# The end of an encoder layer: moved outputs, a wait split over eight chunks, and an embedding product behind the second gate product

## The reference

```python
    x = x + rms_norm(m @ w_out, post_g)

    x = x + jax.nn.sigmoid(x @ w_pg) * (p_i @ w_pe)
    return x
```

## Time and profile before

| | us |
|---|---|
| median of 3 runs | 1331.39 (1331.17 to 1331.68) |
| the profiled execution | 1330.88 |
| its span, first to last instruction | 1329.1 |
| PE busy | 1305.7 |
| DVE busy | 726.3 |
| ACT busy | 596.4 |
| POOL busy | 354.2 |

### The profile page before, as it was taken

One profiled execution on the slowest core, in us unless ns is written; L12 is line 12 of the kernel. 1 busy time (PEld: TensorE's weight loads), 2 busy tenths in 40 slices (PEclk: granted clock), 3 DMA queues, 4 the chain that ended last, 5 costly groups with the idle time before them and its releaser, 6 DMA issues.

```text
span 1329.1 us, 17627 instructions
## 1 busy us (share of the span) xinstructions
PE 1305.7 (98%) x6600; PEld 1065.2 (80%) x6600; DVE 726.3 (55%) x1356; ACT 596.4 (45%) x1152; POOL 354.2 (27%) x239
## 2 busy tenths in 40 slices
PE   9999999999999999999999999999999999999898
PEld 6788877888888778788888788888877888887787
DVE  6354645546522677786633435555547337436865
ACT  6355455553222577676422245555554223224442
POOL 4122212122434311130244512221211443216000
PEclk9999999999999999999999999999999999999999
DMA  6211112101111200000111211111101114424111
GB/s 214 64 41 41 44 38 57 52 32 52 49 48 32 66 31 17 17 17 24 46 53 37 79 52 44 48 50 46 32 24 41 48 40 149 142 79 145 48 40 56
DMA packets 26866, 74.29 MB, mean 56 GB/s; under 512 B 2936, under 2 KB 4856, under 8 KB 26656
## 3 DMA queue, kind: packets, MB, share of 16 engines
q1 hardware_dynamic: 26784, 73.19, 17.4%
HBM read 68.95 MB, written 4.23 MB: 55 GB/s over the span
## 4 chain that ended last, share of the span: by engine, by line
PE 88%; DVE 6%; ACT 3%; issue 2%; DMA 1%; POOL 1%; SPq 0%; ACTq 0%; DVEq 0%; POOLq 0%
PE ps L984 18%; PE ps L1003 14%; PE ps L1340 13%; PE ps L1578 6%; PE ps L1225 6%; PE ps L1392 5%; PE ps L1640 4%; PE ps L1381 2%; PE ps L1023 2%; PE ps L1162 2%; PE ps L1078 2%; PE ps L1310 2%; PE ps L1456 2%; PE ps L1193 1%; PE ps L1284 1%
## 5 line engine op out<-in xcount | busy, mean ns | idle before, releaser
L776 POOL TENSOR_TENSOR w_lo<-stage,w_hi 128x1024 fp32r<-128x1024 f32 (+2 forms) x84 | 190.1, 2264 | 578.9 <-ACT w_hi L1715 578.9
L1715 ACT CAST w_hi<-stage 128x1024 fp32r<-128x1024 f32 (+2 forms) x92 | 91.3, 993 | 198.8 <-PE ps L984 126.4
L2343 DVE TENSOR_TENSOR pt_lo<-ps,pt_hi 128x512 fp32r<-128x512 f32 (+2 forms) x160 | 97.1, 607 | 80.5 <-ACT pt_hi L2079 40.2
L1003 PE MATMUL ps<-h_hi,w_hi 128*128 128x512 f32 x272 | 110.3, 405 | 0.0
L984 PE MATMUL ps<-h_hi,w_hi 128*128 128x512 f32 x352 | 109.0, 391 | 1.2 <-POOL w_lo L776 1.2
L984 PE MATMUL ps<-h_lo,w_hi 128*128 128x512 f32 x352 | 108.5, 389 | 0.0
L984 PE MATMUL ps<-h_hi,w_lo 128*128 128x512 f32 x352 | 108.4, 389 | 0.0
L1340 PE MATMUL ps<-h_hi,w_hi 128*128 128x512 f32 x256 | 106.8, 417 | 0.0
L1003 PE MATMUL ps<-h_hi,w_lo 128*128 128x512 f32 x272 | 106.2, 391 | 0.0
L1003 PE MATMUL ps<-h_lo,w_hi 128*128 128x512 f32 x272 | 106.1, 390 | 0.0
L1340 PE MATMUL ps<-h_hi,w_lo 128*128 128x512 f32 x256 | 100.4, 392 | 0.0
(11 more groups left out here) (456 smaller groups left out, 3131.9 us busy)
## 6 DMA issues: line engine op xcount, KB each, us to landing
stage<-in_w_gates SPq DMA_DIRECT2D x24, 512.0 KB, 3.6
stage<-in_w_qkvg_a SPq DMA_DIRECT2D x19, 512.0 KB, 4.3
stage<-in_w_qkvg_c SPq DMA_DIRECT2D x16, 512.0 KB, 3.7
m<-in_x_tok SPq DMA_DIRECT2D x8, 512.0 KB, 6.1
stage<-in_w_branch SPq DMA_DIRECT2D x8, 512.0 KB, 3.7
y_plain<-in_x_tok SPq DMA_DIRECT2D x8, 512.0 KB, 3.6
stage<-in_w_pg SPq DMA_DIRECT2D x16, 256.0 KB, 3.5
out<-y_plain SPq DMA_DIRECT2D x16, 256.0 KB, 2.0
```

The costliest lines, as they stand in the source:

```text
L776: nc.gpsimd.tensor_tensor(dst, stage[:, staged, 0:width], f32(hi), ALU.subtract).then_inc(w_ready, 1)
L1003: done = mm(ps[:, half_bank(T), :], w[:, slot, k * P:(k + 1) * P], h[:, k, g * SEQ:(g + 1) * SEQ], start=k == 0 and part == 0, stop=k == K ...
L1715: nc.scalar.copy(dst, stage[:, staged, 0:width]).then_inc(w_hi_done, 1)
L2343: sub = lambda out, whole, hi: nc.vector.tensor_tensor(out, whole, f32(hi), ALU.subtract)
```

## The change

On PE the single wait for the right half of w_pg goes. Product e = 2 waits chunk by chunk instead, and all four full gate products go through their chunks in the order PG1_ORDER. In the seven products `gate_embedding(p, 0)` moves from behind the third product to behind the second. On ACT the tanh of e = 1 moves from behind the copies of all weight sums to behind those of c = 0, and the tanh of e = 3 moves ahead of the third unit part and the save of a21. On DVE output 0 moves ahead of weight sums 1, output 1 ahead of weight sums 2 and 3, and output 3 ahead of the third unit part.

```diff
                 pe.wait_ge(o_ready, LEAD + max(e - 1, 0))
-                for k in range(KC):
+                for n, k in enumerate(PG1_ORDER):
+                    if e == 2:
+                        pe.wait_ge(pg1_ready, LEAD + n + 1)
                     for part, (a, w) in enumerate([(a_hi, g_hi), (a_hi, g_lo), (a_lo, g_hi)]):
                         mm(ps[:, c, :], a[:, k * P:(k + 1) * P], w[:, k * 512:(k + 1) * 512],
-                           start=k == 0 and part == 0, stop=k == KC - 1 and part == 2)
+                           start=n == 0 and part == 0, stop=n == KC - 1 and part == 2)
...
-                for i in range(3):
+                for i in range(2):
                     gate_product(p, i)
                 gate_embedding(p, 0)
-                for i in range(3, 5):
+                for i in range(2, 5):
                     gate_product(p, i)
...
             for e in range(PLAIN_EMBEDS):
-                if e == 2:
-                    pe.wait_ge(pg1_ready, LEAD + KC)
                 if e < 3:
                     turn_x2(e + 1)
                 embed(e)
...
                 for which in (4, 2, 3):
                     sums_hi(which, c)
-            embed_tanh(1)
+                if c == 0:
+                    embed_tanh(1)
             unit_hi(0, 0)
             unit_hi(0, 1)
             for t in (2, 3):
                 p_hi(t)
             embed_tanh(2)
+            embed_tanh(3)
             unit_hi(0, 2)
             save_a21(0)
-            embed_tanh(3)
...
             gate_weight_sums(0)
+            output(0, 2)
             gate_weight_sums(1)
-            output(0, 2)
+            output(1, 3)
             gate_weight_sums(2)
             gate_weight_sums(3)
             sums_lo(4)
-            output(1, 3)
             sums_lo(2)
             unit_low(0, 0)
             unit_low(0, 1)
             for t in (2, 3):
                 p_low(t)
             output(2, 2)
+            output(3, 3)
             unit_low(0, 2)
-            output(3, 3)
```

## The result

| | kernel before | changed kernel |
|---|---|---|
| median of 22 runs each, us | 1331.16 | 1333.68 |
| lowest to highest, us | 1330.47 to 1332.35 | 1332.45 to 1334.66 |
| ratio to before (95% interval) | | 1.0018 (1.0012 to 1.0024) |
| profiled execution, us | 1330.88 | 1333.37 |
| its span, us | 1329.1 | 1331.6 |

The first view is what PE waited for in the changed kernel, from 1200 us to the end (engine and line, what it waited for: us in total, times, longest). It answers the earlier trace rows. Lines behind the edits have moved by one to two: the seven products are now L1642, the full gate products L1614, take is L3017, and the output's two operations are L3025 and L3028.

A forecast was written before the change was run, and what follows sets the result against it. TensorE (PE), busy 98% of the span, was taken as the bound. Gains 1.9 + 0.6 against 3.05 added gave 0.55 slower; with 1.4 for the clock, 1331.4 + 0.55 + 1.4 = 1333.4 us, range 1331.0 to 1335.0.

The forecast's parts named there:

- Parts 1 and 2: POOL wait moved chunk-wise into product e = 2; outputs moved up on DVE: gains 1.9 + 0.6 = 2.5 us.
- the full 5.7 of idle time: PE's four waits before the fourth tile's turn, e = 2, e = 3 and the second product: about 5.7 us winnable.
- the later end: Output 0's second operation on DVE takes turns with POOL and ends at 1226.25, instead of 1225.87.
- Part 3: Embedding product behind the second of the seven products: PE waits for take three times, 1.02 each, 3.05 us added.
- the restarts of the waits that go: PE's restarts, each with a slower first matmul, stay at four; 0.1 slower each was allowed in the upper bound.
- the 1.4 for the fall: PE's clock falls in the new 3.85 us wait before the first product: 1.4 us added, middle of nothing and 2.8.
- The bound of 2.8: Upper limit for the clock's cost, from the kernel's start: 20 matmuls took 7.33 us instead of 4.5.
- The argument that the clock had held through 2.20: Support for the clock-holds rival: full 2.4 GHz over 1226 to 1250, through PE's idle gap of 2.20 us.
- That the clock holds: Rival: no clock fall in the long wait before the first product; 1331.9 us (1331.4 to 1332.3), chance 0.30.
- That DVE isn't the bound: Rival: only take's wait is left, 5.7 idle goes and 3.05 comes: 1328.7 us, or 1325.7 with take hidden; chance 0.09.
- The late refill: Rival: the refill for the last quarter of weight sums lands late, DVE and PE lose 1.2: 1334.6 us, chance 0.13.

The follow-up runs named there:

- the changed one without part 3 and without the fall: Changed kernel with the embedding product back behind the third product and 14 matmuls without use in the long wait: 1328.82 us, ratio 0.9982.
- Part 1 alone: Kernel before with only the chunk-by-chunk wait for POOL in product e = 2 and the new chunk order: 1331.21 us, ratio 1.0000.
- part 3 undone: Changed kernel with the embedding product put back behind the third product, everything else still moved: 1330.64 us, ratio 0.9994.
- the filled one: Changed kernel with 14 matmuls without use in the long wait before the first of the seven products: 1331.99 us, ratio 1.0007.
- part 3 alone: Kernel before with only the embedding product moved from behind the third product to behind the second: 1334.72 us, ratio 1.0028.
- the two kernels with output 2 first: Changed kernel, embedding product back behind the third, output 2 ahead of low parts on DVE: 1326.95 us; with two more blocks exchanged: 1325.43 us.

## Why the prediction was right

**The time.** 1333.4 was forecast, 1333.68 measured, with the median of before at 1331.16 instead of 1331.39. The change in time is 2.5 us, with an interval of 1.6 to 3.2, where the sum gave 1.95. All signs that it named came: no wait before the turn, e = 2 and e = 3, one of 3.88 before the first product, three behind take, and a clock of 0.65 behind the long one.

**Parts 1 and 2: right.** 2.5 was forecast; the difference between the kernel before (1331.3) and the changed one without part 3 and without the fall (1328.82) is 2.5, by the median spans 2.8. That it is not the full 5.7 of idle time followed from one reading, that DVE has no idle entry between the first waits and output 2. Output 2 came at 1244.6 in the time of the kernel before, as forecast, and the new wait was 3.88 long (3.85 forecast). Part 1 alone changed nothing (1331.21): it removes a wait behind which another stood. Part 2 without part 1 was not run. By the rows, the wait of 3.88 would have taken up the 1.08 for POOL, so part 1 seems to bring nothing beside part 2 either, which is argued and not shown.

**DVE and POOL: the later end was right.** Output 0's second operation took 1.08 instead of 0.69, the 0.4 that the row of a sum beside POOL had suggested. The Trainium skill (SBUF — State Buffer, Who interferes with whom) has it that a VectorE instruction contends with GpSimd's reads of SBUF when it has two SBUF inputs, and not with at most one. The trace agrees: the first operation with its PSUM input took 0.67 beside POOL, the second with two SBUF inputs waited.

**Part 3: 3.05 forecast, 3.04 measured**, by taking it out of the changed kernel. In the kernel before it costs 3.4, with the part of the fall named above. The profiled executions give a little more. From the turn of the third tile (1218.48 in the earlier trace rows) to the last matmul PE takes 106.21 in the kernel before, 108.32 in the changed one (1218.85 to 1327.17) and 104.96 with part 3 undone (1219.15 to 1324.11), so the three stops cost 3.36. Of that 0.3 is the slower first matmul behind each stop (0.34 to the next start instead of 0.23), which the prediction had set against the restarts of the waits that go.

**The clock: right in kind, too small in size.** The term of the sum that was mis-sized is the 1.4 for the fall. Filling the wait gave 1.7 back with part 3 in place and 1.8 without it, by the median spans 2.0 and 2.1; between the profiled executions of the changed kernel and the filled one it is 1.64 (106.68 from turn to last matmul when filled, 1218.72 to 1325.40). The middle between nothing and 2.8 was a choice, and that it came so near is in part luck. Its reason, that the low level can have begun before the wait ends, is not what the traces show: the clock was at 1.00 through the wait, and all of the low level fell on matmuls, as it did with part 3 undone (1.00 up to 1245.38, where PE goes on, then starts 0.43 apart). The bound of 2.8 is weak too. At the kernel's start the matmuls are slow, but the window shows the clock at 1.00, so that they are slow by the clock isn't shown:

```profile
0.00:4.00 4.00, 2.55 (x6) 2.07 (x7) 0.48 (x1) 0.38 (x1) 0.29 (x5) 1.00 0.53 169
```

The argument that the clock had held through 2.20 was weaker than it looked, since it rested on one execution: with part 3 alone the same two gaps let it fall. The Trainium skill (TensorE: Matmul & The Clock Gate, Why this matters for your kernels) warns of idle gaps between bursts of matmuls, behind which the clock is at half. The changed kernel's 3.88 and the 0.65 behind it agree, and the fill with 14 matmuls shows the price. That the clock fell with gaps of 1.11 and 2.20 too goes further than that warning, which is of longer gaps; there the run decides.

**The rivals.** That the clock holds fell with the 0.65. That DVE isn't the bound fell with the 3.88 released by L3028. The late refill did not come: the weight sums of the last quarter follow on DVE without an idle entry, and the eight loads took 2.6 to 4.6 us to land.

**What the prediction didn't see** is how little was needed. It said that the list on DVE is long and not only in a poor order. The list was long, but 6.7 us of what stood ahead of output 2 (the low parts of two sums, two unit parts and the features, 1236.93 to 1243.62) could come after it. Put in the order of need, the same work gives 5.9 us (1331.30 to 1325.43).

## What to carry to other kernels

A wait of the bounding engine is removed only if the operation that ends it comes earlier on its own engine; moving work that stands behind the same list only moves the wait, so count what is queued ahead of the last releaser and ask of each item when it is needed. An instruction that reuses a bank belongs at least one product behind the one that fills it, or the read in between is exposed in full (0.7 us of reading cost 1.0 us each time). Several short gaps drawn together into a long one can cost more than their sum: behind each of them TensorE's clock can fall, and behind the last one no wait is left that gives the loss back. A few matmuls without use in the gap tell what that share is.

## What the runs showed of the hardware

- TensorE's clock can fall at short gaps. With part 3 alone it fell to half level in the second of two gaps of 1.11 and 2.20 with eight transposes between; in the profiled execution of the kernel before, the same gaps left it at 1.00. So one profile doesn't say whether the clock holds. Of the 54 executions of the kernel before that ran beside the experiments, 23 had a mean granted clock of 0.998 or less, of the 22 of the changed kernel 18, of the 12 of the two kernels with output 2 first none.
- A clock of 1.00 over a gap doesn't show that the gap was harmless. In the changed kernel it was 1.00 through the 3.88 and the slow matmuls came from 1246.16 on, some 1 us after PE had gone on at 1245.07; with part 1 alone they came from 1231.31 on, behind a gap of 3.49 that ended at 1230.49. The starts of the matmuls behind the gap show it.
- A fall costs only what no later wait takes up. With part 1 alone 1.6 us were lost in e = 2 and given back by the wait behind it (0.41 instead of 1.98); ahead of the seven products, with no wait behind, 1.7 to 2.0 were lost in full.
